# Attention in float32r pairs: queries' rope folded, keys' high and low parts stacked in one tile, five score terms, turns ahead of value products

## The reference, cut to what matters

```python
q = (rms_norm(c_q, g_cq) @ w_uq).reshape(B, L, 8, 128 + 64)
q_nope, q_rope = q[..., :128], q[..., 128:]
q_rope = apply_rope(q_rope, cos, sin)            # 64 numbers: a rotation of the pairs (i, i + 32)
k_nope, v = ...                                   # 128 + 128 per head, from c_kv
k_rope = apply_rope(k_rope_raw, cos, sin)         # one for all heads
s = (q_nope . k_nope + q_rope . k_rope) * (128 + 64) ** -0.5
p = softmax(s, axis=-1);  o = p @ v
```

## Time and profile before

| | us |
|---|---|
| median of 3 runs | 2361.85 (2361.36 to 2363.72) |
| profiled execution | 2363.38 |
| its span, first to last instruction | 2361.2 |
| attention, first projection to last product | 974.4 to 1483.3 |
| PE busy in the span | 2224.8 (94%) |
| DVE, ACT, POOL busy | 1056.8, 921.0, 481.1 |
| mean granted PE clock | 0.979 of 2.4 GHz |

### The profile page before, as it was taken

One profiled execution on the slowest core, in us unless ns is written; L12 is line 12 of the kernel. 1 busy time (PEld: TensorE's weight loads), 2 busy tenths in 40 slices (PEclk: granted clock), 3 DMA queues, 4 the chain that ended last, 5 costly groups with the idle time before them and its releaser, 6 DMA issues. The chain is left out here.

```text
span 2361.2 us, 32357 instructions
## 1 busy us (share of the span) xinstructions
PE 2224.8 (94%) x11876; PEld 1860.7 (79%) x11876; DVE 1056.8 (45%) x1711; ACT 921.0 (39%) x1454; POOL 481.1 (20%) x229
## 2 busy tenths in 40 slices
PE   5999999999999999889999998789999999999996
PEld 4988888888888887777777777577888788878785
DVE  5003675675675664366666665364533101421102
ACT  4223354354354354444444444444343223222222
POOL 3110000000000000211111110114444444444443
PEclk8999999999999999999999998899999999999998
DMA  3212121011111111301111110442233233333333
GB/s 146 78 53 63 33 67 63 31 60 61 39 58 62 40 58 46 118 14 46 46 45 45 45 45 27 173 151 81 98 133 98 90 107 107 120 129 98 94 103 123
DMA packets 78713, 182.61 MB, mean 77 GB/s; under 512 B 6864, under 2 KB 27664, under 8 KB 78128
## 3 DMA queue, kind: packets, MB, share of 16 engines
q1 hardware_dynamic: 78640, 181.61, 23.5%
HBM read 152.09 MB, written 29.49 MB: 77 GB/s over the span
## 5 line engine op out<-in xcount | busy, mean ns | idle before, releaser
L1779 POOL TENSOR_TENSOR w_lo<-w_raw,w_hi 128x1024 fp32r<-128x1024 f32 x136 | 330.9, 2433 | 398.6 <-ACT w_hi L1788 398.6
L83 PE MATMUL h_bank<-hn_hi,w_hi 128*128 128x512 f32 (+2 forms) x952 | 374.2, 393 | 4.0 <-PEq L165 2.5
L84 PE MATMUL h_bank<-hn_lo,w_hi 128*128 128x512 f32 (+2 forms) x952 | 356.7, 375 | 0.0
L85 PE MATMUL h_bank<-hn_hi,w_lo 128*128 128x512 f32 (+2 forms) x952 | 356.4, 374 | 0.0
L83 PE MATMUL f_bank<-ffn_in_hi,w_hi 128*128 128x512 f32 x768 | 303.5, 395 | 17.8 <-DVE ffn_in_lo L1968 11.0
L84 PE MATMUL f_bank<-ffn_in_lo,w_hi 128*128 128x512 f32 x768 | 301.4, 392 | 0.0
L85 PE MATMUL f_bank<-ffn_in_hi,w_lo 128*128 128x512 f32 x768 | 301.3, 392 | 0.0
L83 PEld LDWEIGHTS h_bank<-hn_hi,w_hi 128*128 128x128 f32 x952 | 179.6, 189 | 36.7 <-issue 9.9
L85 PEld LDWEIGHTS h_bank<-hn_hi,w_lo 128*128 128x128 f32 x952 | 179.4, 188 | 29.8
L84 PEld LDWEIGHTS h_bank<-hn_lo,w_hi 128*128 128x128 f32 x952 | 179.6, 189 | 28.0 <-issue 3.8
L1788 ACT CAST w_hi<-w_raw 128x1024 fp32r<-128x1024 f32 x136 | 142.7, 1050 | 130.4 <-PE f_bank L85 127.7
(11 more groups left out here) (333 smaller groups left out, 4403.8 us busy)
## 6 DMA issues: line engine op xcount, KB each, us to landing
w_raw<-in_w_ffn SPq DMA_DIRECT2D x136, 512.0 KB, 3.5
w_raw<-in_w_hgrn SPq DMA_DIRECT2D x54, 512.0 KB, 3.6
w_raw<-in_w_out SPq DMA_DIRECT2D x15, 512.0 KB, 4.0
w_raw<-in_w_head SPq DMA_DIRECT2D x9, 512.0 KB, 5.6
X<-in_x SPq DMA_DIRECT2D x8, 520.0 KB, 6.5
values<-v_stage SPq DMA_DIRECT2D x32, 128.0 KB, 1.7
values_h<-values SPq DMA_DIRECT2D x8, 512.0 KB, 4.8
gate_out<-raw SPq DMA_DIRECT2D x8, 512.0 KB, 2.9
```

The lines of the kernel that those rows point to most:

```text
L83: pe.matmul(out, wh, xh, start=start, stop=False)
L84: pe.matmul(out, wh, xl, start=False, stop=False)
L85: return pe.matmul(out, wl, xh, start=False, stop=stop)
L1779: pool.tensor_tensor(w_lo[i][:], w_raw[i][:], w_hi[i][:].bitcast(F32), ALU.subtract).then_inc(w_lo_done, 1)
```

## The change

1. The queries' rope is folded: a float32 matmul with the constant `fold` sums rows r and r + 64 of `q_turned` into `o_bank` (`fold`, L1466 of the new file). ACT takes the high part of all 128 rows (both halves the same), DVE the low part of rows 0 to 63; rows 64 to 127 of the low part are zeroed once at the start. POOL no longer has a part in it.
2. The keys' rope is one tile `kr` instead of two: rows 0 to 63 hold the high part, rows 64 to 127 the low part. So high(q) against `kr` gives high*high and high*low in one matmul, and low(q) against it low*high. A score has five terms instead of six.
3. In `score_head` all `nope` terms of both column parts come first, then the rope terms.
4. Tile 8 is handled on all 128 rows (its other value rows are zero).
5. `turn(2j+2)` stands ahead of `multiply(2j)`, `turn(2j+3)` ahead of `multiply(2j+1)`.
6. Both projections `nope` and `rope` stand ahead of turns 0 and 1, and `fold` behind them. On DVE `q_turned` goes ahead of the low parts 0 and 1.

```diff
+        self.kr = sb("kr_pair", [P, L], F32R)
...
-                            act.copy(hi["kr"][:, 0, a:a + w], bank[x][:, 0:w]).then_inc(hi_done["kr"], 1)
+                            act.copy(lat.kr[:, a:a + w], bank[x][:, 0:w]).then_inc(hi_done["kr"], 1)
...
+                    low = slice(P - ROPE, P)
+                    dve.tensor_tensor(lat.kr[low, a:a + w], bank[x][low, 0:w], lat.kr[low, a:a + w].bitcast(F32),
                                       ALU.subtract).then_inc(lo_done["kr"], 1)
...
-        BEFORE_TURN, AFTER_TURN = (range(4), range(5, 6)), (range(4, 5), range(6, 7))
+        OF_SEGMENT = (range(5), range(5, 7))
...
+                pool.wait_ge(cleared, 2)
+                for half in range(2):
+                    pool.memset(q_rope["lo", half][ROPE:P, :].bitcast(F32), 0.0).then_inc(cleared, 1)
...
-                def rope_part(p, i):
-
-                    piece_hi.wait(pool, p, 5 + 2 * i)
-                    pool.tensor_tensor(q_rope["lo", i][:], q_turned[:], q_rope["hi", i][:].bitcast(F32),
-                                       ALU.subtract).then_inc(rope_lo.sem, 1)
...
+                def fold_high(p, half):
+                    fold_done.wait(act, p, half + 1)
+                    act.copy(q_rope["hi", half][:], o_bank[:]).then_inc(fold_hi.sem, 1)
...
+                def fold_low(p, half):
+                    fold_hi.wait(dve, p, half + 1)
+                    dve.tensor_tensor(q_rope["lo", half][0:ROPE, :], o_bank[0:ROPE, :],
+                                      q_rope["hi", half][0:ROPE, :].bitcast(F32), ALU.subtract
+                                      ).then_inc(fold_lo.sem, 1)
...
                 def segment(cur, nxt, p, which):
                     if p is not None:
-                        for i in BEFORE_TURN[which]:
+                        for i in OF_SEGMENT[which]:
                             piece(p, i)
                     if cur is not None:
                         low(cur, 0)
                         low(cur, 1)
                     if p is not None:
-                        for i in AFTER_TURN[which]:
-                            piece(p, i)
+                        fold_low(p, which)
...
+                def fold(p, half, cur):
+
+                    piece_read.wait(pe, p, 5 + 2 * half)
+                    fold_lo.wait(pe, p, half)
+                    if cur is not None:
+                        h, i = cur
+                        gated.wait(pe, h, i)
+                    pe.matmul(o_bank[:], t.const("fold"), q_turned[:], start=True, stop=True
+                              ).then_inc(fold_done.sem, 1)
...
+                    for n, (q, k) in enumerate((("hi", "hi"), ("hi", "lo"), ("lo", "hi"))):
+                        pe.matmul(out, q_nope[q, i][:, qs], k_nope[k, par][:, a:a + w], start=(n == 0), stop=False)
...
+                    pe.matmul(out, q_rope["hi", i][:, qs], kr[:, a:a + w], start=False, stop=False)
+                    return pe.matmul(out, q_rope["lo", i][:, qs], kr[:, a:a + w], start=False, stop=True)
...
+                    for part in parts:
+                        nope_terms(nxt, j, *part)
+                    if j == 0:
+                        fold_lo.wait(pe, x, i + 1)
+                    for part in parts:
+                        last = rope_terms(nxt, j, *part)
+                    last.then_inc(head_done.sem, 1)
...
-                def multiply(cur, k):
+                def multiply(cur, k, p=None):
...
+                        if p is not None:
+                            fold_lo.wait(pe, p, i + 1)
...
                         if cur is not None:
-                            multiply(cur, 2 * j)
                             turn(cur, 2 * j + 2)
+                            multiply(cur, 2 * j, p)
                         if nxt is not None:
                             score_tail(nxt, j)
                         if cur is not None:
-                            multiply(cur, 2 * j + 1)
                             if 2 * j + 3 < TILES:
                                 turn(cur, 2 * j + 3)
+                            multiply(cur, 2 * j + 1)
```

More of the change, by code:

```diff
@@ L951, in latents @@
         rs = {n: sb(f"rs_{n}", [P, width[n]]) for n in ("ckv", "cq")}
-        hi = {n: lat.parts[n, "hi"] for n in width}
-        lo = {n: lat.parts[n, "lo"] for n in width}
+        hi, lo = ({n: lat.parts[n, x] for n in ("ckv", "cq")} for x in ("hi", "lo"))
         turned = sb("kr_turned", [P, L])
@@ L987, in _ @@
             def _(pool):
-                for n in ("ckv", "kr"):
-                    for part in (hi[n], lo[n]):
-                        pool.memset(part[:, :, L:].bitcast(F32), 0.0).then_inc(padded, 1)
+                for part in (hi["ckv"], lo["ckv"]):
+                    pool.memset(part[:, :, L:].bitcast(F32), 0.0).then_inc(padded, 1)
                 for b in range(2):
@@ L1114, in attention_heads @@
         cq, ckv = ({x: lat.parts[n, x] for x in both_parts} for n in ("cq", "ckv"))
-        kr = {x: lat.parts["kr", x][:, 0, :] for x in both_parts}
+        kr = lat.kr
         table = lat.table
@@ L1152, in attention_heads @@
         NP_ = len(PIECES)
-        BEFORE_TURN, AFTER_TURN = (range(4), range(5, 6)), (range(4, 5), range(6, 7))
+        OF_SEGMENT = (range(5), range(5, 7))
+        BY_ACT = [i for i, piece in enumerate(PIECES) if not piece[0].startswith("rope")]
         def signal(name, per):
@@ L1169, in attention_heads @@
         mixed_out = [signal(f"mixed_out{i}", 16) for i in range(2)]
-        def rows(k):
-            return slice(0, P) if k < TT else META_ROWS
         def iterations(eng, both):
@@ L1253, in both @@
                         if p is not None:
-                            rope_part(p, which)
                             if which == 0:
@@ L1285, in piece @@
                     s_done.wait(act, p, (half + 1) * QS, lag=1)
-                    if name.startswith("nope"):
-                        piece_done.wait(act, p, i + 1)
-                        act.copy(q_nope["hi", half][:], src).then_inc(piece_hi.sem, 1)
-                    else:
-                        piece_read.wait(act, p, i + 1)
-                        act.copy(q_rope["hi", half][:], q_turned[:]).then_inc(piece_hi.sem, 1)
+                    piece_done.wait(act, p, i + 1)
+                    act.copy(q_nope["hi", half][:], src).then_inc(piece_hi.sem, 1)
+                def fold_high(p, half):
+                    fold_done.wait(act, p, half + 1)
+                    act.copy(q_rope["hi", half][:], o_bank[:]).then_inc(fold_hi.sem, 1)
                 def values(p):
@@ L1326, in segment @@
                     if p is not None:
-                        for i in AFTER_TURN[which]:
-                            piece(p, i)
+                        fold_high(p, which)
                     for j in range(QS):
@@ L1361, in piece @@
                     if name.startswith("nope"):
-                        piece_hi.wait(dve, p, i + 1)
                         dve.tensor_tensor(q_nope["lo", half][:], src, q_nope["hi", half][:].bitcast(F32),
@@ L1366, in piece @@
                         piece_done.wait(dve, p, i + 1)
-                        rope_lo.wait(dve, p, half)
+                        fold_done.wait(dve, p, half)
                         dve.tensor_tensor(q_turned[:], src, table[:, a:a + w],
                                           ALU.mult).then_inc(piece_read.sem, 1)
+                def fold_low(p, half):
[3 more added lines that the diff above has]
+                                      ).then_inc(fold_lo.sem, 1)
                 def find_top(nxt, j):
@@ L1464, in project, with nope_terms @@
                     last.then_inc(piece_done.sem, 1)
-                def terms(nxt, j):
+                def fold(p, half, cur):
[6 more added lines that the diff above has]
+                              ).then_inc(fold_done.sem, 1)
+                def nope_terms(nxt, j, out, a, w):
                     x, i = nxt
@@ L1470, in terms, with rope_terms @@
                     qs = slice(j * P, (j + 1) * P)
-                    return [(q_nope["hi", i][:, qs], k_nope["hi", par]), (q_nope["hi", i][:, qs], k_nope["lo", par]),
-                            (q_nope["lo", i][:, qs], k_nope["hi", par]), (q_rope["hi", i][:, qs], kr["hi"]),
-                            (q_rope["hi", i][:, qs], kr["lo"]), (q_rope["lo", i][:, qs], kr["hi"])]
-                def score(nxt, j, out, a, w):
-                    for n, (q, k) in enumerate(terms(nxt, j)):
-                        last = pe.matmul(out, q, k[:, a:a + w], start=(n == 0), stop=(n == 5))
-                    return last
+                    for n, (q, k) in enumerate((("hi", "hi"), ("hi", "lo"), ("lo", "hi"))):
+                        pe.matmul(out, q_nope[q, i][:, qs], k_nope[k, par][:, a:a + w], start=(n == 0), stop=False)
+                def rope_terms(nxt, j, out, a, w):
+                    x, i = nxt
+                    qs = slice(j * P, (j + 1) * P)
```

(5 more changed lines are left out.)

39 lines of the change are left out of this document (21 added, 18 removed).

## The result

The kernel after ran in 2336.74 us (median of 4 runs, 2329.80 to 2340.77), the kernel before beside it in 2362.78 (4 runs, 2361.36 to 2367.01). The ratio is 0.9888, with an interval of 0.9874 to 0.9902. That is 26.0 us less (23 to 30 by the interval) where 19.8 were forecast. The profiled execution took 2335.76 us, 27.6 less than the one of before, with a span of 2334.0 and a granted clock of 0.980. The first page line of the profile after (busy time, share of the span, instructions) shows how little of this the totals tell: PE's share rises.

What follows compares the result with a forecast made beforehand. DVE's 5.35 us round was taken to set the pace within segments, PE at their openings. Fourteen segments -18.5, first head +1.5, last opening -1.5, last segment -1.3 gave -19.8 us: 2342 us, range 2332 to 2354.

Steps and rivals of the forecast that it cites:

- Rounds 1 and 2: Mid-segment, from one DVE `shift` to the next: stays 5.35 us, so the five terms gain nothing there.
- the fold's low part hidden: At segment openings, the chain fold, ACT, DVE ends before `top` 0 wants DVE, with 0.45 us to spare.
- the step from `top` to `low`: On DVE at openings, `low` 2 starts 1.06 us after `top` instead of 1.75, as turn 2 precedes the product.
- the first head's +1.5: First head, with no products to hide anything: two folds +1.9, one shorter head -0.375, together +1.5 us.
- a larger total wait of PE in the attention: Sign of being right: PE's total wait in the attention grows although the time is shorter.
- The openings: Between one segment's last `shift` and the next's first: -6.5 us in seven first segments, -9.5 in seven second ones.
- Tile 8 in a second segment: End of a second segment, 128 rows instead of 32: only one DVE step counts, -0.12 us; PE's restart -0.11.
- The last segment: Only turns and products: earlier turns save 1.2 us (0 to 2.4), with tile 8's 0.12 together -1.3 us.
- The last opening: Last head's opening, without projections and at half clock: one term less, earlier turn and tile 8, -1.3 us in the table.
- A: Whole attention: PE's work counts everywhere, so the rounds get shorter too; -30 us, 2332 us; chance 0.11.
- B: Segment openings do not get shorter, since fold chain or tail scores end late; -6 us, 2356 us; chance 0.14.
- C: Openings: granted clock falls to 1.2 GHz, work takes 1.84 times as long; slower, 2400 us; chance 0.05.

Runs made afterwards that it cites:

- experiment 1: Kernel after with the low(q) rope term multiplied twice, so a score has six matmuls again: 2342.42 us, ratio 0.9910.
- experiment 3: Kernel after with the fold matmul issued twice in each opening: 2351.76 us, ratio 0.9947.
- experiment 6: ACT's high part ahead of the exponentials, one DVE low part moved into its wait for ACT: kernel after 2310.61 us, kernel before 2347.03 us.
- experiment 2: First, kernel after with turns behind the products again: 2345.76 us; second, kernel before with only the turns moved ahead: 2347.16 us.
- experiment 4: Kernel after with rope projected behind turns 0 and 1 again and `q_turned` behind low parts 0 and 1: 2348.61 us, ratio 0.9928.
- experiment 5: Kernel after with tile 8's copies and product back on its last 32 rows: 2339.44 us, ratio 0.9895.
- the third kernel of experiment 6: Kernel after with the low part moved into DVE's wait and the low(q) rope term multiplied twice: 2331.16 us, ratio 0.9856.

## Why the prediction was right

**What held.** Rounds 1 and 2 at 5.35 us on DVE with one wait of 1.53, PE's block at 4.65, the fold at 0.43 per record, the fold's low part hidden, the step from `top` to `low` at 1.05 (1.06 forecast): each is in a row above. So is, in the table, the first head's +1.5, which is 1.35 counted from its first projection. Experiments 1, 3 and 6 took the rounds and the fold one by one, and each stood; experiments 2 and 4 did it for the turns.

**Signs that did not come.** I had named a larger total wait of PE in the attention as a sign of being right. It fell: by the busy time in the windows from the first projection to the last product, PE is idle 41.5 of 508.9 us before and 34.8 of 481.3 after. The sign was at odds with my own sum, in which PE loses 15.1 us of work (30.3 less 15.2) and the kernel 19.8. And PE does not wait 0.7 us in every block. It runs ahead, waits 0.26 in the third block, and most of its wait, 0.91 and 0.51 by the rows above, stands before the products of the last two tiles.

**What was mis-sized, all to the same side.** In three of the five the granted clock has a part that is no part of the mechanism.
- *The openings.* From the last `rope` matmul to the fold I had 1.27, it is 1.19. It is not the turns that make this: without them it is 1.18 (experiment 4); why the fold starts 0.08 sooner behind the projection than the head did stays open. From there to the end of the head 2.815, it is 2.74. Together 0.155 per opening, 2.2 us in 14. Second openings show most of it (12.27 - 10.80 = 1.47, forecast 1.36). First openings show less: in three of the seven `q_turned` came some 0.1 us later and the fold began 1.44 to 1.46 after the last `rope` matmul, with a wait of 0.18, which makes them 14.62 instead of 14.36.
- *The two openings of 13.45.* 2.3 us of the gain between the two profiles are not the change. In the profiled run of before, PE ran twice for 3.4 us at half clock in the `nope` projection of a second segment; rows below.
- *Tile 8 in a second segment.* I let only one of its two steps of 0.12 count. Both lie between `top` and `shift`; round 3 gained 0.27, not 0.12, 1.1 us in seven. Experiment 5 confirms 0.25.
- *The last segment.* Forecast -1.3, measured -3.0, above even the upper bound of 2.4 that I had for the turns. Two things are in it. The turns are worth (2.81 - 2.28)/2 = 0.265 per tile at full clock, 1.86 in seven, where I had taken 1.2; experiment 2 takes back just that, 18.85 - 16.99 = 1.86. The other 1.1 us are the clock's: PE was back at full clock 6.0 us after the segment's first turns, before it took 8.3. It is not the turns that bring this, since two kernels with the turns behind the products had full clock back within 6.0 us as well: experiment 2's first took 18.85 us and the kernel before with the edit of experiment 6 18.86, where the profile of before shows 19.97.
- *The last opening.* Forecast -1.3, measured -2.1: the first transposes, 1.97 us at half clock before, ran at full clock this time (1.12 us), and the clock fell only after them, for 3.4 us instead of 6.8. In experiment 5 the same opening ran with 6.8 us of half clock and took 10.46, 1.3 less than before. So the forecast held for equal clock, and the other 0.8 were luck.

The clock makes up 2.3 + 1.1 + 0.8 = 4.2 us of the 27.5 between the two profiles. Without it they would differ by 23.3, which is 3.5 more than forecast. Whether the 26.0 us between the medians hold as much of it is not shown, since only one run of each kernel has a profile.

**The rivals.** A, PE counts everywhere: falsified by rounds of 5.35 and by experiment 1. It was the right law for another kernel, the one with the shorter DVE chain. That the median came even a little nearer to its 2332 (4.7 us) than to my 2342 (5.3) is no support: its 14 us of rounds are not there, and the nearness is chance. B, the opening not shorter: the fold's chain ended 0.47 us ahead of `top`, no opening was late. C, half clock in all openings: the granted clock over one and a half heads is 1.00, though PE now waits within segments too (busy time by engine, clock, DMA share and GB/s, of the stretch of the earlier trace rows and of one and a half heads):

```profile
core 0: us, PE busy (x) PEld busy (x) DVE busy (x) ACT busy (x) POOL busy (x), PEclk, DMA share, GB/s
1000.00:1005.00 5.00, 2.64 (x15) 2.20 (x15) 3.31 (x6) 2.45 (x6) 2.42 (x1) 1.00 0.02 3
1112.00:1174.00 62.00, 58.87 (x332) 49.41 (x331) 41.30 (x85) 29.53 (x66) 7.63 (x4) 1.00 0.14 44
```

PE is busy 2.64 us of 5 in the first head now, 0.5 less than before, still at 1.00. But right behind this stretch, from 1007 to 1011 us in the key projection, the granted clock was 0.57, after PE had stood still from 1004.1 to 1006.4. Before, it was 1.00 there. The change did not bring this: the kernel before with the edit of experiment 6 has such a stretch too, and it cost nothing that shows, since this opening is 1.04 us shorter, like the others. C's factor of 1.84 was a wrong reading that came out right by chance: 0.427 and 0.232 us are a float32 and a float32r matmul, both at full clock, while the rows of half clock below give 0.43 against 0.23. The Trainium skill's rule of an engine that swings between half and full clock in short pauses ("TensorE: Matmul & The Clock Gate", section "A second HAM failure mode: psum-queue depth-cycling") did not bear on these rounds, though single stretches like it do occur, as the next part but one shows.

## What to carry to other kernels

Fewer matmuls pay only where TensorE's own block is the longest chain: find the pace by the distance between two starts of the same instruction on each engine. The engine that waits only inside its own loop (here VectorE for ScalarE's exponentials of the same block) sets it. In an interval bound by another engine's wait, move that engine's work into the wait first; the same saving on TensorE that was worth 6 us here was worth 21 after six lines were moved. And put work that is ready (turns) into the waits for what is not (a rope table's product) before counting what a new step costs: the fold's 0.95 us per opening were nearly paid by it.

## What the runs showed of the hardware

**Half clock in one execution and not in the next.** TensorE in the kernel before, the start of a `nope` projection:

```profile
1222.59 0.63 PE L84 MATMUL a_scores<-cq_lo,w_hi 128*128 128x512 f32 x1
1223.02 0.63 PE L85 MATMUL a_scores<-cq_hi,w_lo 128*128 128x512 f32 x1
...
1226.95 0.39 PE L84 MATMUL a_scores<-cq_lo,w_hi 128*128 128x512 f32 x1
1227.18 0.39 PE L85 MATMUL a_scores<-cq_hi,w_lo 128*128 128x512 f32 x1
```

Equal matmuls stand 0.43 us apart at 1222.59 and 0.23 at 1226.95, and the granted clock of 1222 to 1226 is 0.57. Ahead of it PE had waited 0.45 and 0.65 us, as it does in every segment. In the openings between the second head's first and the last head's first, the profile of before has two such stretches, experiment 5 has one, and the ten others have none, the kernel after among them. One costs 1.2 to 1.5 us in an opening. So a single profiled run can be off by 2 or 3 us, and a difference of this size between two profiles needs its own cause shown.

**A `shift` of 0.65 us.** The same VectorE instruction on 128x1 takes 0.22 us, or 0.65 as at 1148.97 above, once in a first segment. GpSimd's row at that time:

```profile
1146.94 2.66 POOL L1244 TENSOR_TENSOR v_lo<-raw,v_hi 128x1152 fp32r<-128x1152 f32 x1 [18.16 <-ACT v_hi L1292]
```

It ends at 1149.60, and the `shift` at 1149.62. In the kernel before it is the `shift` at 1154.57, 0.70 us, with `v_lo` from 1152.54 to 1155.26: again both end together. All twelve profiles show this in all seven first segments, and the two never end more than 0.03 us apart. The earlier the `shift` starts within `v_lo`, the longer it takes: 1.91 us behind its start it took 0.78 (1140.34 in experiment 6), 2.03 behind it 0.65, while `v_lo` itself takes 2.65 to 2.72. So the `shift` seems to wait for the end of `v_lo`. It costs the round 0.4 us in seven segments of the kernel after, and nothing where PE's 5.12 sets the round (the third kernel of experiment 6). No run took GpSimd's work away, so that it is the cause is likely, not shown.

**32 rows are slower than 128.** A VectorE low part of 32 rows starts 0.12 us later behind its neighbour and delays the next by 0.12, though it takes as long (0.70 and 0.68). On TensorE, the product of tile 8 and what follows it took 0.88 us from its first matmul to the projection's first, against 0.80 with 128 rows, and the step inside the projection behind it 0.34 against 0.25.
